# Gates of the mixers as tokens by 512 columns from split parts, with filler kept for the later attentions

## What is computed

```
for l in range(DEPTH):                      # DEPTH = 2, float32
    h = rmsnorm(x, norm1_g[l])              # 256 x 1024
    z = h @ w_in[l]                         # 1024 x (2520 + 4096)
    z_mla, z_nsa, z_fox, z_dsa, z_gate = split_cols(z, ...)
    o_mla, o_nsa = mla_mixer(z_mla, ...), nsa_mixer(z_nsa, ...)
    o_fox, o_dsa = fox_mixer(z_fox, ...), dsa_mixer(z_dsa, ...)
    branches = jnp.stack([o_mla, o_nsa, o_fox, o_dsa], axis=2)      # 256 x 4 x 256
    lifted = jnp.einsum('bsnc,ncd->bsnd', branches, w_branch[l])    # 256 x 4 x 1024
    gates = jax.nn.sigmoid(z_gate.reshape(B, S, 4, 1024))
    mixed = jnp.sum(gates * lifted, axis=2)
    x = x + mixed @ w_out[l]
    h2 = rmsnorm(x, norm2_g[l])
    x = x + jnp.square(jax.nn.relu(h2 @ w_up[l])) @ w_down[l]
```

## Time and profile before

| | us |
|---|---|
| three runs | 1690.52, 1694.66, 1699.96 |
| median | 1694.66 |
| profiled execution | 1691.54 |
| its span, first to last instruction | 1689.8 |
| PE busy | 1577.7 (93%) |
| DVE busy | 766.8 (45%) |
| ACT busy | 683.1 (40%) |
| mean granted clock of PE | 0.974 of full |

### The profile page before, as it was taken

One profiled execution on the slowest core, in us unless ns is written; L12 is line 12 of the kernel. 1 busy time (PEld: TensorE's weight loads), 2 busy tenths in 40 slices (PEclk: granted clock), 3 DMA queues, 4 the chain that ended last, 5 costly groups with the idle time before them and its releaser, 6 DMA issues.

```text
span 1689.8 us, 23874 instructions
## 1 busy us (share of the span) xinstructions
PE 1577.7 (93%) x9950; PEld 1316.6 (78%) x9950; DVE 766.8 (45%) x1480; ACT 683.1 (40%) x1025; POOL 435.3 (26%) x163
## 2 busy tenths in 40 slices
PE   5999889997998999989999889999999998899997
PEld 4867767864997778578888668999888886689996
DVE  2734677423766764163342463522433522635222
ACT  3334466422436654152223353444432233454442
POOL 1200034320000443133000034655531000246543
PEclk9999989998997999999999999999999999999999
DMA  9597379678625786743424144555443332346550
GB/s 386 191 330 269 133 267 347 238 272 326 242 95 200 264 309 233 294 180 137 141 100 175 50 167 157 185 190 180 167 169 129 116 150 75 118 162 207 183 191 26
DMA packets 46620, 327.26 MB, mean 194 GB/s; under 512 B 5424, under 2 KB 5424, under 8 KB 8752
## 3 DMA queue, kind: packets, MB, share of 16 engines
q1 hardware_dynamic: 46512, 325.73, 53.5%
HBM read 324.66 MB, written 1.05 MB: 193 GB/s over the span
## 4 chain that ended last, share of the span: by engine, by line
PE 79%; DVE 13%; ACT 3%; DMA 3%; issue 1%; POOL 1%; DVEq 0%; SPq 0%; ACTq 0%
PE ps L201 28%; PE ps L204 16%; PE ps L206 16%; PE ps L205 16%; DVE lo L212 5%; DMA raw<-in_wmod 2%; ACT hi L209 1%; PE ps L2624 1%; DVE ar L212 1%; DMA raw<-in_wo_v 1%; DVE big L220 1%; POOL lo L212 1%; DVE xn L212 1%; DVE gl L212 1%; PE ps L989 1%
## 5 line engine op out<-in xcount | busy, mean ns | idle before, releaser
L212 POOL TENSOR_TENSOR lo<-raw,hi 128x2048 fp32r<-128x2048 f32 (+2 forms) x76 | 354.4, 4673 | 638.8 <-ACT hi L209 638.8
L209 ACT ACTIVATE hi<-raw 128x2048 fp32r<-128x2048 f32 (+2 forms) x192 | 350.8, 1858 | 48.4 <-PE ps L206 12.5
L212 DVE TENSOR_TENSOR lo<-raw,hi 128x2048 fp32r<-128x2048 f32 (+1 forms) x116 | 291.4, 2529 | 102.5 <-ACT hi L209 102.3
L201 PE MATMUL ps<-hT,raw 128*128 128x256 f32 x1024 | 231.4, 382 | 0.0
L201 PEld LDWEIGHTS ps<-hT,raw 128*128 128x128 f32 x1024 | 191.2, 190 | 29.4 <-issue 3.9
L204 PE MATMUL ps<-hTh,hi 128*128 128x256 f32 x640 | 183.2, 286 | 5.4 <-DVE hTl L212 2.9
L205 PE MATMUL ps<-hTl,hi 128*128 128x256 f32 x640 | 182.5, 285 | 0.0
L206 PE MATMUL ps<-hTh,lo 128*128 128x256 f32 x640 | 182.4, 285 | 0.0
L204 PEld LDWEIGHTS ps<-hTh,hi 128*128 128x128 f32 x640 | 124.2, 194 | 7.1 <-issue 3.5
L204 PE MATMUL ps<-hi,hTh 128*128 128x512 f32 (+3 forms) x320 | 119.0, 372 | 10.7 <-DVE hTl L212 5.2
L205 PEld LDWEIGHTS ps<-hTl,hi 128*128 128x128 f32 x640 | 124.1, 194 | 0.5
(11 more groups left out here) (297 smaller groups left out, 2535.2 us busy)
## 6 DMA issues: line engine op xcount, KB each, us to landing
raw<-in_wgu SPq DMA_DIRECT2D x64, 1024.0 KB, 5.0
raw<-in_wmod SPq DMA_DIRECT2D x48, 1024.0 KB, 6.4
raw<-in_wdn SPq DMA_DIRECT2D x32, 1024.0 KB, 5.6
raw<-in_wgt SPq DMA_DIRECT2D x32, 1024.0 KB, 4.9
raw<-in_wup SPq DMA_DIRECT2D x32, 1024.0 KB, 4.8
raw<-in_wdown SPq DMA_DIRECT2D x32, 1024.0 KB, 5.3
raw<-in_wz SPq DMA_DIRECT2D x12, 1024.0 KB, 4.9
raw<-in_wbr SPq DMA_DIRECT2D x8, 1024.0 KB, 5.7
```

What stands on the lines that cost most here:

```text
L201: return self.e.matmul(o, l, r, start=first, stop=last)
L209: return self.e.activation(o, a, f, **kw)
L212: return self.e.tensor_tensor(o, a, b, op)
```

## The change

Gate weights are laid out as 1024 rows by 512 columns, in chunks of 128 x 1024 (half a slot). A gate step is now a quarter of a group: four products of 128 tokens by 512 columns by 128 rows, each as `mm3` from split parts, 12 matmuls; a group has four steps and fills banks 6 and 7 (pool C), one for each half of the tokens. ACT makes the high part and DVE the low part, `ahead=2`: in step j they make the parts of step j+2. Results stand as tokens by columns, so the norm can be a scale by partition: ACT's tanh takes `scale=half_rstd`, and `divisors` and `v_divide` go. `enter_gates` cuts three raw slots into six halves, keeps one whole slot, and cuts hTat's buffer and one hi buffer into four half hi buffers; probabilities lie in raw slot 4, transposed ones behind `z`.

Lifts are tokens by 512 columns too, in banks 6 and 7. The mixed sum must therefore be transposed before `wo`: `t_mix_T`, sixteen transposes in two halves, with the parts made out of PSUM. The attentions' transposes and products use banks 2 to 5 (pool N) and scores always banks 0 and 1. Two filler steps stand ahead of the heads, and the first two weaves call the filler through `paced` with 3 of 4 turns, so that 25 gate steps stand before the third weave and 7 in it.

```diff
+RMIX = 4
@@ Book
+    def enter_gates(self):
+        self.epoch += 1
+        *halved, whole = [r for r in self.rings["R"] if r < RMIX]
+        self.rings["R"] = [whole]
+        self.rings["Q"] = [NR + 2 * r + i for r in halved for i in range(2)]
+        self.rings["H"] = [NH + i for i in range(4)]
...
-    POOLS = dict(A=(0, 4), B=(4, 4), G=(4, 2), C=(6, 2), S=(0, 2), M=(2, 2))
+    POOLS = dict(A=(0, 4), B=(4, 4), G=(4, 2), C=(6, 2), S=(0, 2), M=(2, 2), N=(2, 4))
...
     def pair(self, *key):
-        turn = self.book.turn
-        b = 0 if turn["A"] in (0, 3) else 2
-        turn["A"] = (b + 2) % 4
-        self.use(b, *key, 0)
-        self.use(b + 1, *key, 1)
-        return b
+        self.use(0, *key, 0)
+        self.use(1, *key, 1)
+        return 0
...
+def paced(step, a, b):
+    n = 0
+    def filler():
+        nonlocal n
+        n += 1
+        for _ in range(n * a // b - (n - 1) * a // b):
+            step()
+    return filler
...
+PACE = (3, 4), (3, 4)
...
-            if i == 2:
-                b = t.take("B", "divisors", l)
...
     def t_fill(self, t, l):
-        for d in range(8):
-            for n in range(4):
-                if n % 2 == 0:
-                    c = t.chunk("gt", l, d, n // 2)
-                    wv = kn(c.raw, 8)
-                b = t.take("B", "gate", l, d, n)
...
-                for k in range(8):
-                    m = t.mm(self.ps[:, b, 0:256], wv[:, k, 128 * (n % 2):128 * (n % 2) + 128], self.hT[:, k, :],
-                             k == 0, k == 7)
+        for g in range(8):
+            banks = [t.take("C", "gate", l, g, q) for q in range(2)]
+            for i in range(4):
+                c = t.chunk("gt", l, g, i)
+                wh, wl = kn(c.hi, 2), kn(c.lo, 2)
+                t.wait_ge(*t.at("lo", c.key))
+                for q, b in enumerate(banks):
+                    if i == 0:
+                        t.wait_ge(*t.free(b))
+                    for k in range(2):
+                        m = t.mm3(self.ps[:, b, :], [h[:, 2 * i + k, 128 * q:128 * q + 128] for h in self.H3],
+                                  (wh[:, k, :], wl[:, k, :]), i == k == 0, i == 3 and k == 1)
...
+            for h, q in self.QUARTERS:
+                b = t.take("C", "lift", l, n, h, q)
...
+                for k in range(2):
+                    m = t.mm(self.ps[:, b, :], V.oTs[:, n, k, 128 * q:128 * q + 128], wv[:, k, 512 * h:512 * h + 512],
+                             k == 0, k == 1)
...
+                if i == 3 and (h, q) == (1, 0):
+                    self.t_mix_T(t, l, n, 0)
...
     def a_fill(self, a, l):
+                self.a_split(a, "gt", l, g, i, ahead=2)
+                if i == 3:
...
+                        a.ac(V.sg[:, g // 2, q, 512 * (g % 2):512 * (g % 2) + 512], self.ps[:, b, :], ACT.Tanh,
+                             scale=self.half_rstd()[:, q:q + 1]).then_inc(*a.up(f"free{b}"))
...
     def v_fill(self, v, l):
+                self.v_split(v, "gt", l, g, i, ahead=2)
...
     def t_mixers(self, t, l):
+        step()
+        step()
         for _ in self.t_heads(t, l):
             step()
-        weave([self.t_indexer(t, l), self.t_compress(t, l)], 2, step)
+        weave([self.t_indexer(t, l), self.t_compress(t, l)], 2, paced(step, *PACE[0]))
...
-               self.t_attend(t, l, "nwin", nq, kk(1), keys, nsa_values), self.t_latent(t, l)], 3, step)
+               self.t_attend(t, l, "nwin", nq, kk(1), keys, nsa_values), self.t_latent(t, l)], 3, paced(step, *PACE[1]))
```

More of the change, by code:

```diff
@@ L43 @@
 SEMS.update({f"free{b}": f"the last reader of bank {b} has emptied it" for b in range(8)})
-SEMS.update({f"raw{r}": f"a chunk of weights landed in slot {r}" for r in range(NR)})
+SEMS.update({f"raw{r}": f"a chunk of weights landed in slot {r}" for r in range(NR + 2 * RMIX)})
 SMALL = ("sil", "cst", "col", "x", "cx", "row", "pos", "gb00", "gb01", "gb10", "gb11", "fg")
@@ L2125, in a_z @@
             self.a_split(a, "z", l, i, 1)
+            if i == 5:
+                for k in range(4):
+                    a.wait_ge(*a.at("hT", ("c", l), k))
+                self.a_split(a, "gt", l, 0, 0, ahead=1)
             b = a.bank("z", l, i, 1)
@@ L2180, in t_fill @@
                 t.mark("mixers done", l)
-                t.book.leave("mixers done", l)
-            for d in range(0, 8, 2):
-                b = t.take("B", "lift", l, n, d)
+                t.book.leave("mixers done", l, first=RMIX)
+            for h, q in self.QUARTERS:
+                b = t.take("C", "lift", l, n, h, q)
                 t.wait_ge(*t.at("landed", c.key))
@@ L2206, in a_fill @@
                 yield
-            n = a.lifts.pop(0)
-            for d in range(0, 8, 2):
+            a.lifts.pop(0)
+            for h, q in self.QUARTERS:
+                if i == 2 and (h, q) == (1, 1):
+                    self.a_split(a, "wo", l, 0, 0, ahead=0)
                 if i == 3:
-                    if d == 0:
-                        a.wait_ge(*a.at("mixers done", l))
-                        self.a_split(a, "wo", l, 0, 0, ahead=0)
+                    if (h, q) == (0, 0):
                         a.wait_ge(*a.at("lifted", l, 2))
@@ L2228, in v_fill @@
             n = v.lifts.pop(0)
-            for d in range(0, 8, 2):
-                b = v.bank("lift", l, n, d)
-                g2 = V.sg[:, n, d:d + 2, :]
-                v.wait_ge(*v.empty("gate", l, 7, 3))
-                v.wait_ge(*v.full("lift", l, n, d))
-                v.stt(g2, g2, 1.0, two(self.ps[:, b, :]), ALU.add, ALU.mult).then_inc(*v.up(f"free{b}"))
+            for h, q in self.QUARTERS:
+                b = v.bank("lift", l, n, h, q)
+                g2 = V.sg[:, n, q, 512 * h:512 * h + 512]
+                v.wait_ge(*v.empty("gate", l, 7, 1))
+                v.wait_ge(*v.full("lift", l, n, h, q))
+                v.stt(g2, g2, 1.0, self.ps[:, b, :], ALU.add, ALU.mult).then_inc(*v.up(f"free{b}"))
@@ L2248, in v_fill, with v_mix @@
                 yield
             v.before = n
+    def v_mix(self, v, l, h):
+        for kp in (2 * h, 2 * h + 1):
+            b = v.bank("mix T", l, kp)
+            v.wait_ge(*v.at("part hi", "mT", l, kp))
+            v.tt(self.H3[1][:, 2 * kp:2 * kp + 2, :], two(self.ps[:, b, :]),
+                 self.H3[0][:, 2 * kp:2 * kp + 2, :].bitcast(F32), ALU.subtract).then_inc(*v.up(f"free{b}"))
+            v.mark("mT", l, kp)
     def g_fill(self, g, l):
         V = self.views2()
-        for d in range(8):
-            for n in range(4):
+        for gg in range(8):
+            for i in range(4):
+                self.g_split(g, "gt", l, gg, i, ahead=2)
@@ L2453, in t_compress @@
         V, ps = self.views2(), self.ps
[L2454 to L2456 removed]
+        b = t.take("N", "cmp in", l)
         t.wait_ge(*t.at("rope", l))
@@ L2465, in t_compress @@
         yield
-        b = t.take("B", "cmp", l)
+        b = t.take("N", "cmp", l)
+        c = t.chunk("cmp", l)
+        wv = c.raw.rearrange("p (s m d) -> p s m d", s=2, m=16)
         t.wait_ge(*t.at("windows", l))
@@ L2475, in t_compress @@
         yield
-        b = t.take("B", "cmp k", l)
+        b = t.take("N", "cmp k", l)
         t.wait_ge(*t.empty("cmp", l))
@@ L2738, in t_latent @@
         V, ps = self.views2(), self.ps
-        wm = t.chunk("mla", l)
         yield
         for i in range(3):
-            b = t.take("B", "cT", l, i)
+            b = t.take("N", "cT", l, i)
             t.wait_ge(*t.at("latent", l))
@@ L2748, in t_latent @@
         yield
+        wm = t.chunk("mla", l)
         t.wait_ge(*t.at("landed", wm.key))
         for q in range(2):
-            b = t.take("B", "mla q", l, q)
+            b = t.take("N", "mla q", l, q)
             t.wait_ge(*t.empty("cT", l, 2))
```

211 lines of the change are left out of this document (121 added, 90 removed).

## The result

The changed kernel takes 1706.1 us (median of 5; 1703.6 to 1711.7), the kernel before, beside it, 1695.4. The ratio is 1.0072, 95% interval 1.0052 to 1.0092: slower by 0.7%, where 10 us less was forecast. The profiled execution has a span of 1703.9 us in place of 1689.8, so 14.1 more where the sum said 10 less: 24 us to explain.

A forecast was written before the change was run, and what follows sets the result against it. PE, busy for 93% of the span, was taken as the bound. Per layer -16.9, +11.3 and +1.1 gave -4.5, -10 for both; from the median of 1694.66 this made 1685 us (forecast case 1672 to 1698, whole range 1646 to 1708).

The forecast's parts named there:

- the sum: Per layer -16.9 for the first part, +11.3 for the second, +1.1 in the output product: -4.5; -10 for both layers.
- the row: Profile row of eight transposes between other PE work, 1.04 us; from it sixteen new transposes per layer were booked at +2.1.
- the seven items: Waits of PE at chains in each layer's first part, from the stage's start to the long rows' first transposes: together 25.8 us.
- -2.1 (the slow clock, whose wait is filled): Second part of a layer: PE gets back 2.1 us lost to the slow clock behind the old 4.66 us wait.
- The wait at 957: PE's old 4.66 us wait for a DVE and ACT chain in a layer's second part; forecast to go.
- 8.3 - 11.5 in the second: Second part of a layer: 8.3 us of forecast waits, against 11.5 us of idle time of PE before.
- -25.6 us per layer: Gates on PE: 32 old steps of 3.52 us, 112.6, become 32 new ones of 2.72 us, 87.0.
- the clock falls: Rival, 20%: PE's clock drops behind the new waits, five a layer losing 10.5 us; -4.5 to +6.0 per layer, 1707 us.
- "+1.1" for the output product: The second eight transposes of a layer stand inside the output product and add 1.1 us.

The follow-up runs named there:

- the filled waits: Changed kernel with products nobody reads put into four long waits of PE per layer: 1701.5 us, ratio 1.0051 against the kernel before.
- the early low part: Changed kernel with DVE making the low part of the output product's second chunk ahead of the last mixed tokens' low parts: 1697.2 us, ratio 1.0040.
- the 16 us for layout and banks: Changed kernel with gate products float32 again, new layout, banks, transposes and kept steps staying: 1685.2 us, against 1669.3 for the kernel before with kept steps alone.

## Why the prediction was wrong, by its own steps

**Right.** The rate of gate products within a step, the low parts' length, the transfers, and most waits of the first part with their releaser. The eight new transposes at 1004.20 took 1.03 us, as the row had it (0.13 us each) and not as 275 ns each would have. In the first layer they were, in the order of the seven items, against the forecast in brackets: 0.7 (1.0), 1.7 (2.5), 3.1 (3.4), 1.7 and a wait of 2.05 for the gate's banks that I had not seen (3.4), 4.4 (6.2), 0.4 and 1.7 (3.0 and 1.8), 3.5 and 0.9 (4.1 and 0.4). That is 20.2 us in place of 25.8. From the end of z's products to the latent attention's first scores (at 918.4 us, 932.8 before) it took 125.4 us in place of 139.0: 13.6 less, where 16.9 were forecast. That this is so near is in part luck: waits booked 5.6 us too long stand against 4.7 that the clock lost and some 4 that the 25 steps took beyond 2.72 us each.

**The step that failed: "-2.1 (the slow clock, whose wait is filled)".** The sum booked the clock as a gain of 2.1 us a layer and left what twelve new waits do to it to a rival with one chance in five. The wait at 957 was filled, and one of 3.37 us at the forgetting attention took its place. The first layer's second part, from the latent scores to the output product, grew by 16.2 us (63.8 to 80.0) where 11.3 were forecast: of the 4.9 us of miss the clock is 2.7 (it lost 2.75 us, as against 2.2 before, and was to lose nothing), and waits are most of the rest (10 us in place of 8.3). Over both layers the clock was booked at -4.2 and came to +16.5: 20.7 of the 24 us. Here are the three terms of the sum, for both layers from the mixers' start to the feed-forward part. The forecast of the idle time is 25.8 - 1.6 us a layer in the first part and 8.3 - 11.5 in the second.

| | forecast, us | measured, us |
|---|---|---|
| PE's work at full clock (gates, transposes) | -47 | -39 |
| PE's idle time | +42 | +37.5 |
| the clock's loss | -4.2 | +16.5 |

**A term that was mis-sized: "-25.6 us per layer" for the gates.** It took the step as 12 adjacent products and so as 2.72 us. With 2.85 it is 32 x 0.67 = 21.4, which is 4.2 us a layer less. The waits, which were booked too long, hide half of that in the total.

**The rival that came true.** In form the result is the rival "the clock falls", with the time that I gave for it, 1707; it had 10.5 us a layer of loss, and 9.2 and 12.5 were measured. That the time agrees to 1 us is luck as well, since the gates' and the idle time's errors nearly cancel. I held the rival down because DVE would absorb the loss. How much it absorbs in the changed kernel stays open, for the filled waits are not clear of the noise; in the kernel before, where 5.2 us of loss were removed, the two stages became 4.0 us shorter and the ratios give 6.8 (4.2 to 9.3), so little was absorbed there. A loss of 2.1 us behind one wait of 4.66 was in the earlier trace rows, and the sum had six waits of 3 us or more a layer.

**A term that was mis-sized: "+1.1" for the output product.** It counted the transposes as PE work and did not look at what they do to DVE's order. From the product's start to the feed-forward part the first layer took 32.9 us in place of 28.6: 4.3, of which the early low part gave back most (a wait 2.7 us shorter and 1.7 of the clock's loss).

**A question not asked.** All parts were added up at once. The kept steps were booked with their waits in the new form, where they cost (1699.9 without them), and so it stayed hidden that on the kernel before they are worth 24.5 us. There the first part's chains have 3.52 us a step, nothing of the gates on DVE, and 25 steps still cover them.

**What stays open.** Of the 16 us for layout and banks, some 5 are the late low part and 4.2 the transposes, and 7.3 by another count are the clock; which of the fixed pair, the two gate banks and other waits makes the remainder was not told apart. Low parts give 45 us when removed but only 7 when half of them go to GpSimd: the 32 us by which DVE's other operations became longer explain this in size, but which waits of PE they made was not followed. Where the clock falls changes from kernel to kernel and single gains of 4 to 7 us have intervals of 4 to 5, so they are not to be added up.

## What to carry to other kernels

An operation moved to an engine with spare time is free only if it doesn't stand, in that engine's order, between two links of a chain that the bound engine waits for; count it in each link, not in the busy share. Price each new wait of PE with the slow clock behind it, and ask of each part of a change what it would do alone: filler kept for late chains was worth 1.5% by itself (24.5 us), and the layout and the split products that it was bundled with cost 37 us. Where a late wait can't be filled with work, unread products in it can pay.

## What the hardware showed that I had not expected

- Products that nobody reads, 3.5 us in a wait of 4.66, made the kernel before faster by 0.4% (0.25 to 0.55%).
- The granted clock stood at 0.50 (846 to 852 us in the run with filled waits) after nothing longer than pauses of 0.8, 1.3 and 0.45 us in some ten microseconds of otherwise busy PE.
- A two-input DVE operation of 256 columns that began 0.26 us after a two-input GpSimd operation took 2.49 us in place of 0.42; over the kernel, 32 low parts on GpSimd made DVE's other operations some 32 us longer.
- Of 66 us taken from an engine that is busy for half of the span, 45 came out as time.
